# RWKV slot: half of the b Gram product copied by ScalarE, level one's dx in another bank, the v turn first, GpSimd's building a level later

## The chip, the cores and the metric

The program runs on one core of a Trainium2 chip (trn2). The metric is the device time of one launch in microseconds (us), the median of several runs. TensorE (PE) does the matrix products into PSUM, VectorE (DVE), ScalarE (ACT) and GpSimd (POOL) work beside it, and SyncE (SP) issues the loads of the weights. Each engine takes its instructions in the order in which they are written; semaphores hold the engines together.

## The reference, cut to what matters

The model is two blocks of two layers each over 256 tokens of 1024 columns. The change touches only one mixer of the first block, RWKV-7, and within it only the scan over time:

```python
def frame_step(state, inp):
    r_t, w_t, k_t, v_t, a_t, b_t = inp
    sa = jnp.einsum('bhvk,bhk->bhv', state, a_t)
    state = (state * w_t[:, :, None, :]
             + sa[..., None] * b_t[:, :, None, :]
             + v_t[..., None] * k_t[:, :, None, :])
    y_t = jnp.einsum('bhvk,bhk->bhv', state, r_t)
    return state, y_t
```

It is run for 16 heads of 64 columns, in 4 chunks of 64 tokens. The projections before it, the gate, the output product and the MLP behind it are large matrix products.

## The kernel before

The scan is done by chunks instead of by tokens. Within a chunk the dependence of the tokens on each other is a unit lower triangular matrix; its inverse is made first, for all chunks at once, and then a short chain goes from chunk to chunk with the state. Four heads (two pairs, called q = 0 and q = 1) make a **slot**, and there are four slots (`SLOTS`). A fifth pass of the loop holds the last chain.

For a slot `s` there is a list of steps, the same on every engine (`WKV_STEPS`, L572 to L581):

- **gram**, q 0 and 1. TensorE makes the b Gram product (`acc[0]`, `acc[1]`, from `b_fm` and `ar`) at q = 0, and turns v into tokens there (`un`, the v turn); at q = 1 it makes the k Gram product (`acc[2]`, `acc[3]`, from `k_fm` and `ar`). VectorE reads the b Gram product of pair q: `xt` (L1992), the level-one matrix `n_m` (L1993), `xt` plus the unit matrix (L1994), the masked product `nb_t` (L1995, 512 columns), and the transpose `xn` (L1996). ScalarE copies v out (L1281).
- **tok**. TensorE turns b and k into tokens. VectorE masks the k Gram product into `nk_t` (L2000), twice. ScalarE makes the exponentials `w_cum` and `w_inv` of the next slot (`wkv_build`, L1140 and L1141).
- **levels** j = 1 to 5, each with t1 (q 0, 1) and dx (q 0, 1). TensorE: t1 = `n_m` times `xn` into `acc[q]`; ScalarE copies it to `t1` (L1287); TensorE: dx = `xt` times `t1` into the second half of bank `acc[2 + q]`; VectorE adds it into `xt` (L2005) and transposes (L2008). GpSimd makes the `n_m` of levels 2 to 5 from `nb_t` (L817).
- **chain** steps rhs, u, sy, of the slot before, set between these by `WKV_CHAIN_AFTER`. rhs (TensorE) also finishes the y of the chunk before; ScalarE copies it to `wkv_rhs` (L1293); u (TensorE) follows, ScalarE copies it to `wkv_u` (L1301); sy makes the new state and y. VectorE copies y out (`keep_y`, L1980 and L1982), and sy waits for that before it writes y again.

In the code below, a step such as t1 of level 2, pair 1 is ("t1", 2, 1); the text calls it t1 2/1. Since each engine has one order, a step is late when its own input is late or when the instruction ahead of it on its engine is.

GpSimd also builds the operands of the next slot, `b_fm` and `k_fm` (`build_bk`) and `ar` (`build_ar`), between the `n_m` of two levels. In slot 0, which has no chain, TensorE has the last weight units of v beside the levels (L2252 to L2254), and VectorE splits their weights into high and low parts (L1507) and prepares the inputs of later slots (L1882 to L1889).

Of the kernel before, what the change touches and what calls it, by code (L numbers as in the profile page):

```python
# [7 lines left out]
ALU = mybir.AluOpType  # L8
# [5 lines left out]
P = 128  # L14
# [86 lines left out]
def build(nc, A, out):  # L101

    with ExitStack() as ctx:
# [626 lines left out]
        def _(pool):  # L730
# [79 lines left out]
            for s in range(SLOTS):  # L810
                for j in WKV_LEVELS[1:]:
                    for q in range(2):
                        if j == 2:
                            pool.wait_ge(inv_ready, 12 * s + q + 1)
                        else:
                            pool.wait_ge(t1_done, 10 * s + 2 * (j - 3) + q + 1)
                        G.tensor_tensor(n_m[(j - 1) % 2][:, q, :, :], nb_t[s % 2][:, q, :, 0:CHUNK],  # L817
                                        level_t[:, j, :].unsqueeze(1).to_broadcast([P, CHUNKS, CHUNK]), ALU.mult).then_inc(nm_ready, 1)
                    if j == (2 if s else 4) and s + 1 < SLOTS:
                        build_bk(s + 1)  # L820
                    if j == (3 if s else 5) and s + 1 < SLOTS:
                        build_ar(s + 1)
# [43 lines left out]
        def _(act):  # L866
# [618 lines left out]
        def _(dve):  # L1485
# [499 lines left out]
            for slot in range(SLOTS + 1):  # L1985
                for n, (step, s, j, q) in enumerate(wkv_steps(slot)):
                    xt, xn = inv_t[SLOT_SET[s]][:, q, :, :], inv_x[:, q, :, :]
                    if step == "gram":

                        dve.wait_ge(g_done, s + 1)  # L1990
                        raw_n = acc[q][:, :, :].rearrange("p a s -> p (a s)").rearrange("p (c q) -> p c q", c=CHUNKS)
# [5 lines left out]
                    elif step == "tok":  # L1997

                        dve.wait_ge(gk_done, s + 1)
                        V.tensor_tensor(nk_t[s % 2][:, q, :, :], bank4(acc[2 + q]), bc4(c_("masks"), CHUNKS), ALU.mult).then_inc(lak_ready, 1)  # L2000
                    elif step == "dx":
# [3 lines left out]
                        ins = V.tensor_tensor(x_, late(flat(acc[2 + q])[:, 2 * P:4 * P], j), x_, ALU.add)  # L2005
# [3 lines left out]
                        ins.then_inc(inv_ready, 1)  # L2009
                    elif step == "sy":  # L2010
# [236 lines left out]
        def _(pe):  # L2247
# [403 lines left out]
            for slot in range(SLOTS + 1):  # L2651
                for n, (step, s, j, q) in enumerate(wkv_steps(slot)):
# [3 lines left out]
                    if step == "gram":  # L2656
                        if q == 0:
                            pe.wait_ge(built, s + 1)
                            pe.wait_ge(const_mid_in, 16)
                            if s:  # L2660
                                pe.wait_ge(t1_out, 10 * s)
# [4 lines left out]
                            for c in range(CHUNKS):  # L2666
                                for m in range(2):
                                    ins = by_head(bank4(acc[m])[:, c, :], b_fm[:, m, c, :], ar[r_][:, m, c, :], cross=m == 1)
                            ins.then_inc(g_done, 1)
# [4 lines left out]
                            ins.then_inc(v_done, 1)  # L2674
                        else:
                            pe.wait_ge(inv_ready, 12 * s)
# [20 lines left out]
                    elif step == "dx":  # L2697
                        if j == 1:
                            pe.wait_ge(lak_ready, 2 * s + q + 1)
                        pe.wait_ge(t1_out, 10 * s + 2 * (j - 1) + q + 1)  # L2700
                        for c in range(CHUNKS):
                            ins = by_head(late(half_bank(acc[2 + q], 1)[:, c, :], j), t1[:, q, c, :], late(xt[:, c, :], j))
                        ins.then_inc(dx_done, 1)
                    else:
# [4 lines left out]
                        if step == "rhs":  # L2709
                            if c == 0:  # L2710
                                pe.wait_ge(inv_ready, 12 * s + 12)
                                pe.wait_ge(tok_out, 4 * s + 4)
                                pe.wait_ge(lak_ready, 2 * s + 2)
# [314 lines left out]
```

## Time and profile before

| | us |
|---|---|
| median of 3 runs | 1351.38 |
| lowest, highest | 1350.61, 1351.99 |
| profiled execution, its span | 1350.7 |
| the four slots and the last chain (427 to 550) | 123 |
| TensorE busy over the span | 1303.9 (97%) |
| VectorE busy | 948.4 (70%) |
| ScalarE busy | 701.1 (52%) |
| GpSimd busy | 128.3 (9%) |

A row of the timeline has the start in us, the length in us (of a row of several instructions, from the first's start to the last's end), engine, line, operation, output and inputs, shape and count; in brackets stands how long the engine had been idle, and what ended that. TensorE's rows count two instructions where the program has one in 32-bit arithmetic. TensorE's granted clock was 0.998 of its full level (2.4 GHz) on average, and is no part of what follows.

### The profile page before, as it was taken

What the parts mean: (1) busy time and instruction counts of PE and PEld (TensorE: products, weight loads), DVE (VectorE), ACT (ScalarE), POOL (GpSimd) and SP (SyncE); (2) the same over time, 40 slices, a digit from 0 to 9 for tenths busy, and PEclk for the clock granted to TensorE, in tenths of its full rate; (3) what the DMA queues carried; (4) which work ended last, traced back from release to release, by engine and by line L of the source; (5) the groups of instructions that cost most, each with busy time, mean ns of one, the idle gap of its engine ahead of it and who ended that gap; (6) DMA issues with size and microseconds to landing.
All of it is one profiled execution on the core that took longest, in us unless ns stands there. A gap on an engine that the chain in (4) does not pass through costs nothing. (4 is left out here: it accounts for less than half of the span.)

```text
span 1350.7 us, 24951 instructions
## 1 busy us (share of the span) xinstructions
PE 1303.9 (97%) x10507; PEld 1130.7 (84%) x10507; DVE 948.4 (70%) x1433; ACT 701.1 (52%) x1211; POOL 128.3 (9%) x133
## 2 busy tenths in 40 slices
PE   4999999999999999999999999999999999999997
PEld 2998888997899887788888887888888998888886
DVE  1887788976768776685556888666657677756655
ACT  2534544434467455564444648654445566644443
POOL 0000000010200864100000142000000021000000
PEclk9999999999999999999999999999999999999999
DMA  9997899995341012356665532465565544565561
GB/s 363 373 366 236 302 350 381 356 344 161 110 156 64 4 35 97 98 178 196 188 192 177 176 121 74 150 203 192 187 196 160 170 143 126 172 188 192 183 197 51
DMA packets 177559, 256.90 MB, mean 190 GB/s; under 512 B 10472, under 2 KB 122536, under 8 KB 177448
## 3 DMA queue, kind: packets, MB, share of 16 engines
q1 hardware_dynamic: 177448, 255.31, 57.0%
q8 instruction: 83, 1.36, 0.4%
q14 instruction: 28, 0.23, 0.0%
HBM read 254.25 MB, written 1.05 MB: 189 GB/s over the span
## 5 line engine op out<-in xcount | busy, mean ns | idle before, releaser
L1507 DVE TENSOR_TENSOR w_lo<-stage,w_hi 128x1024 fp32r<-128x1024 f32 (+1 forms) x372 | 447.3, 1238 | 160.4 <-ACT w_hi L882 160.0
L882 ACT ACTIVATE w_hi<-stage 128x1024 fp32r<-128x1024 f32 (+1 forms) x378 | 379.9, 1049 | 211.7 <-PE acc L2311 191.9
L2309 PE MATMUL acc<-w_hi,z_hi 128*128 128x512 f32 x640 | 252.7, 395 | 1.6 <-DVE z_lo L1956 1.6
L2311 PE MATMUL acc<-w_hi,z_lo 128*128 128x512 f32 x640 | 249.4, 390 | 0.0
L2310 PE MATMUL acc<-w_lo,z_hi 128*128 128x512 f32 x640 | 249.2, 389 | 0.0
L2252 PE MATMUL un<-h_both,w_hi 128*128 128x256 f32 x736 | 214.9, 292 | 1.8 <-POOL w_lo L853 1.1
L2253 PE MATMUL un<-h_both,w_hi 128*128 128x256 f32 x736 | 208.8, 284 | 0.0
L2254 PE MATMUL un<-h_both,w_lo 128*128 128x256 f32 x736 | 208.8, 284 | 0.0
L2252 PEld LDWEIGHTS un<-h_both,w_hi 128*128 128x128 f32 x736 | 141.6, 192 | 9.5 <-issue 5.4
L2309 PEld LDWEIGHTS acc<-w_hi,z_hi 128*128 128x128 f32 x640 | 120.1, 188 | 27.8 <-issue 3.9
L2253 PEld LDWEIGHTS un<-h_both,w_hi 128*128 128x128 f32 x736 | 141.7, 193 | 1.2 <-issue 0.7
L2254 PEld LDWEIGHTS un<-h_both,w_lo 128*128 128x128 f32 x736 | 141.7, 193 | 0.0
L2311 PEld LDWEIGHTS acc<-w_hi,z_lo 128*128 128x128 f32 x640 | 120.1, 188 | 25.4
L2310 PEld LDWEIGHTS acc<-w_lo,z_hi 128*128 128x128 f32 x640 | 120.2, 188 | 23.4
L2290 PE MATMUL un<-h_both,w_hi 128*128 128x512 f32 x384 | 121.2, 397 | 0.4 <-DVE w_lo L1507 0.4
L2290 PE MATMUL side<-h_both,w_hi 128*128 128x512 f32 x384 | 120.8, 396 | 0.4
L2293 PEld LDWEIGHTS side<-h_both,w_lo 128*128 128x128 f32 x384 | 72.1, 188 | 17.0
L2293 PEld LDWEIGHTS un<-h_both,w_lo 128*128 128x128 f32 x384 | 72.1, 188 | 16.9
L2293 PE MATMUL un<-h_both,w_lo 128*128 128x256 f32 x384 | 75.5, 278 | 0.0
L2293 PE MATMUL side<-h_both,w_lo 128*128 128x256 f32 x384 | 75.5, 278 | 0.0
L1789 DVE SCALAR_TENSOR_TENSOR ada_sum<-ada_buf,small,ada_sum 128x1024 f32<-128x1024 f32 x49 | 62.8, 1282 | 1.0
L2290 PEld LDWEIGHTS un<-h_both,w_hi 128*128 128x128 f32 x384 | 59.1, 189 | 1.7 <-DVE w_lo L1507 0.6
(393 smaller groups left out, 1885.1 us busy)
## 6 DMA issues: line engine op xcount, KB each, us to landing
stage<-in_mlp_w SPq DMA_DIRECT2D x64, 1024.0 KB
ada_buf<-in_ada_w SPq DMA_DIRECT2D x48, 1024.0 KB, 11.1
stage<-in_w_up SPq DMA_DIRECT2D x32, 1024.0 KB
stage<-in_w_down SPq DMA_DIRECT2D x32, 1024.0 KB
stage<-in_conv_w_in SPq DMA_DIRECT2D x12, 1024.0 KB
stage<-in_rw_w_rkv SPq DMA_DIRECT2D x12, 1024.0 KB
stage<-in_w_in_a SPq DMA_DIRECT2D x8, 1024.0 KB
stage<-in_w_kv_b SPq DMA_DIRECT2D x8, 1024.0 KB
```

The costliest lines, as they stand in the source:

```text
L882: A_(w_hi[u % 2][:, half, 0:n], stage[u % NSTAGE][:, half, 0:n], ACT.Copy).then_inc(hi_made, 1)
L1507: V.tensor_tensor(w_lo[u % 2][:, half, 0:n], stage[u % NSTAGE][:, half, 0:n], w_hi[u % 2][:, half, 0:n].bitcast(F32), ALU.subtract).then_i ...
L1789: V.scalar_tensor_tensor(out=to[:], in0=rows, scalar=by, in1=to[:], op0=ALU.mult, op1=ALU.add).then_inc(ada_weighed, 1)
L2252: MM(out, hi_l, hi_r, start=start, stop=False, skip_group_check=True)
L2253: MM(out, hi_l, lo_r, start=False, stop=False, skip_group_check=True)
L2254: return MM(out, lo_l, hi_r, start=False, stop=stop, skip_group_check=True)
L2290: MM(pair[:, m, :, :], wh[:, kt, c], h_both[:, kt, :, :], start=(kt == 0), stop=False, skip_group_check=True)
L2293: ins = MM(pair[:, m, 0, :], wl[:, kt, c], h_hi[:, kt, :], start=False, stop=(kt == KT - 1), skip_group_check=True)
L2309: MM(y, z_hi[:, kt, q], wh[:, i, :], start=(first and kt == 0), stop=False, skip_group_check=True)
L2310: MM(y, z_hi[:, kt, q], wl[:, i, :], start=False, stop=False, skip_group_check=True)
L2311: ins = MM(y, z_lo[:, kt, q], wh[:, i, :], start=False, stop=(last and kt == KT - 1), skip_group_check=True)
```

## The change

- **v turn first.** TensorE makes the v turn ahead of the b Gram product. The b Gram product now waits for `inv_ready` (VectorE's last addition of the slot before), where it had waited for ScalarE's last copy of t1.
- **Half of the b Gram product by ScalarE.** Columns 0 to 63 of each chunk of `nb_t` are no longer masked by VectorE but copied unmasked by ScalarE, pair 1 as soon as the Gram product is there, pair 0 after VectorE has made `xt` and `n_m` from it. VectorE masks only the other half, and for pair 0 it waits for ScalarE's copy. Both v copies of ScalarE stand ahead of it.
- **Level one's dx** goes to the second half of `acc[q]`, and the masking of k (`nk_t`) is moved from ahead of level one to behind each of its additions. TensorE's wait for it is at dx of level two.
- **`wkv_build`** on ScalarE is moved behind level one's copies.
- **GpSimd** starts level two's `n_m` at ScalarE's copies, and in slots 1 and 2 it builds b and k behind level three's `n_m` and ar behind level four's (before: level two's and three's).

```diff
 # GpSimd
                         if j == 2:
-                            pool.wait_ge(inv_ready, 12 * s + q + 1)
+                            pool.wait_ge(tok_out, 4 * s + 2)
...
-                    if j == (2 if s else 4) and s + 1 < SLOTS:
+                    if j == (3 if s else 4) and s + 1 < SLOTS:
                         build_bk(s + 1)
-                    if j == (3 if s else 5) and s + 1 < SLOTS:
+                    if j == (4 if s else 5) and s + 1 < SLOTS:
                         build_ar(s + 1)
 # ScalarE
                     if step == "gram":
-                        act.wait_ge(v_done, s + 1)
-                        act.wait_ge(lo_made, 2 * (BESIDE_SLOT[0] + 1))
-                        A_(v_tok[SLOT_SET[s]][:, q, :, :], half_bank(un[q], 1), ACT.Copy).then_inc(tok_out, 1)
-                    elif step == "tok":
-                        if q == 1 and s + 1 < SLOTS:
-                            wkv_build(s + 1)
+                        if q == 0:
+                            act.wait_ge(v_done, s + 1)
+                            act.wait_ge(lo_made, 2 * (BESIDE_SLOT[0] + 1))
+                            for m in range(2):
+                                A_(v_tok[SLOT_SET[s]][:, m, :, :], half_bank(un[m], 1), ACT.Copy)
+                            act.wait_ge(g_done, s + 1)
+                        else:
+                            act.wait_ge(lak_ready, 3 * s + 1)
+                        A_(nb_t[s % 2][:, 1 - q, :, 0:CHUNK], bank4(acc[1 - q])[:, :, 0:CHUNK], ACT.Copy).then_inc(tok_out, 1)
...
+                            if q == 1 and s + 1 < SLOTS:
+                                wkv_build(s + 1)
 # VectorE
-                        link(V.tensor_tensor(n_m[0][:, q, :, :], raw_n[:, :, 0:CHUNK], bc4(level_t[:, 1, :], CHUNKS), ALU.mult))
+                        ins = V.tensor_tensor(n_m[0][:, q, :, :], raw_n[:, :, 0:CHUNK], bc4(level_t[:, 1, :], CHUNKS), ALU.mult)
+                        if q == 0:
+                            ins.then_inc(lak_ready, 1)
+                            dve.wait_ge(lak_ready, 3 * s + 1)
+                        else:
+                            link(ins)
                         V.tensor_tensor(xt, xt, bc4(eye, CHUNKS), ALU.add)
-                        link(V.tensor_tensor(nb_t[s % 2][:, q, :, :], raw_n, bc4(c_("masks"), CHUNKS), ALU.mult))
+                        dve.wait_ge(tok_out, 4 * s + 2)
+                        link(V.tensor_tensor(nb_t[s % 2][:, q, :, CHUNK:2 * CHUNK], raw_n[:, :, CHUNK:2 * CHUNK], bc4(c_("masks")[:, CHUNK:2 * CHUNK], CHUNKS), ALU.mult))
...
-                        ins = V.tensor_tensor(x_, late(flat(acc[2 + q])[:, 2 * P:4 * P], j), x_, ALU.add)
+                        ins = V.tensor_tensor(x_, late(flat(acc[q if j == 1 else 2 + q])[:, 2 * P:4 * P], j), x_, ALU.add)
...
+                        if j == 1:
+                            dve.wait_ge(gk_done, s + 1)
+                            V.tensor_tensor(nk_t[s % 2][:, q, :, :], bank4(acc[2 + q]), bc4(c_("masks"), CHUNKS), ALU.mult).then_inc(lak_ready, 1)
 # TensorE
-                        if j == 1:
-                            pe.wait_ge(lak_ready, 2 * s + q + 1)
+                        if j == 2:
+                            pe.wait_ge(lak_ready, 3 * s + q + 2)
```

TensorE between slot 1 and slot 2, `un<-const,rw` being the v turn, `ar,b_fm` and `ar,k_fm` the Gram products, `side<-...` chain steps. Before:

```order
L2642 MATMUL acc<-inv_t_128,t_152 64x32 x16
L2642 MATMUL acc<-ar_191,b_fm 64x128 x16
L2642 MATMUL un<-const_64,rw_113 64x64 x16
L2642 MATMUL side<-v_tok_127,nk_t_136 64x64 x4
L2642 MATMUL acc<-ar_191,k_fm 64x128 x16
```

And after:

```order
L2654 MATMUL acc<-inv_t_128,t_152 64x32 x16
L2654 MATMUL un<-const_64,rw_113 64x64 x16
L2654 MATMUL acc<-ar_191,b_fm 64x128 x16
L2654 MATMUL side<-v_tok_127,nk_t_136 64x64 x4
L2654 MATMUL acc<-ar_191,k_fm 64x128 x16
```

The v turn and the b Gram product have changed places; nothing else has on this engine.

VectorE in slot 1, from the second pair's level-one matrix to level one's additions (L1995 and L2000 of before are the two maskings). Before:

```order
L1995 TENSOR_TENSOR nb_t_134<-acc,const_64 128x512
L1996 STREAM_TRANSPOSE inv_x<-inv_t_128 128x256 [waits dve_chain]
L2020 TENSOR_SCALAR state_146<-side,w_end 128x64 [waits s_done]
L2020 TENSOR_SCALAR state_146<-side,w_end 128x64
L2000 TENSOR_TENSOR nk_t_136<-acc,const_64 128x512 [waits gk_done] x2
L2005 TENSOR_TENSOR inv_t_128<-acc,inv_t_128 128x64x2 [waits dx_done]
L2008 STREAM_TRANSPOSE inv_x<-inv_t_128 128x256 [waits dve_chain]
L1980 COPY tmp<-side 128x64 [waits y_done]
L1982 COPY tmp<-side 64x64 x2
L2005 TENSOR_TENSOR inv_t_128<-acc,inv_t_128 128x64x2 [waits dx_done]
```

And after:

```order
L2008 TENSOR_TENSOR nb_t_134<-acc,const_64 128x4x64 [waits tok_out]
L2009 STREAM_TRANSPOSE inv_x<-inv_t_128 128x256 [waits dve_chain]
L2032 TENSOR_SCALAR state_146<-side,w_end 128x64 [waits s_done]
L2032 TENSOR_SCALAR state_146<-side,w_end 128x64
L2014 TENSOR_TENSOR inv_t_128<-acc,inv_t_128 128x64x2 [waits dx_done]
L2017 STREAM_TRANSPOSE inv_x<-inv_t_128 128x256 [waits dve_chain]
L2021 TENSOR_TENSOR nk_t_136<-acc,const_64 128x512 [waits gk_done]
L1985 COPY tmp<-side 128x64 [waits y_done]
L1987 COPY tmp<-side 64x64 x2
L2014 TENSOR_TENSOR inv_t_128<-acc,inv_t_128 128x64x2 [waits dx_done]
```

The masking of the b product has half its columns and a wait; the masking of k has moved from ahead of the first addition to between that and the copies of y.

ScalarE in slot 1, level one. Before:

```order
L1290 ACTIVATE bk_tok_129<-un 128x512 [waits tok_done]
L1293 ACTIVATE wkv_rhs<-side 128x128 [waits rhs_done]
L1298 ACTIVATE state_kept<-state_146,w_end 128x64 [waits state_ready]
L1298 ACTIVATE state_kept<-state_146,w_end 128x64
L1301 ACTIVATE wkv_u<-side 128x128 [waits u_done]
```

And after:

```order
L1293 ACTIVATE bk_tok_129<-un 128x512 [waits tok_done]
L1140 ACTIVATE w_cum<-rw_114 128x512 [waits built]
L1141 ACTIVATE w_inv<-rw_114 128x512
L1298 ACTIVATE wkv_rhs<-side 128x128 [waits rhs_done]
L1303 ACTIVATE state_kept<-state_146,w_end 128x64 [waits state_ready]
L1303 ACTIVATE state_kept<-state_146,w_end 128x64
L1306 ACTIVATE wkv_u<-side 128x128 [waits u_done]
```

The two exponentials now stand ahead of the chain's copy.

## Rows read from the trace of the kernel before

**Rows 1.** Timeline, VectorE, slot 2: start, length, engine, line, operation.

```profile
478.58 0.29 DVE L2005 TENSOR_TENSOR inv_t<-acc,inv_t 128x128 f32<-128x128 f32 x1 [0.41 <-PE acc L2642]
479.52 0.42 DVE L1992 TENSOR_TENSOR inv_t<-acc,const 128x256 f32<-128x256 f32 x1 [0.65 <-PE acc L2642]
479.86 0.41 DVE L1993 TENSOR_TENSOR n_m<-acc,const 128x256 f32<-128x256 f32 x1
...
480.65 0.68 DVE L1995 TENSOR_TENSOR nb_t<-acc,const 128x512 f32<-128x512 f32 x1
481.37 0.45 DVE L1996 STREAM_TRANSPOSE inv_x<-inv_t 128x256 f32<-128x256 f32 x1
...
484.26 1.28 DVE L2000 TENSOR_TENSOR nk_t<-acc,const 128x512 f32<-128x512 f32 x2
```

**Rows 2.** Timeline, TensorE, slot 1.

```profile
462.18 0.68 PE L2642 MATMUL acc<-inv_x,n_m 64*64 64x64 f32 x16 [1.50 <-DVE inv_x L1996]
...
464.01 0.45 PE L2642 MATMUL side<-wkv_rhs,inv_t 64*64 64x64 f32 x8
...
465.46 0.45 PE L2642 MATMUL side<-v_tok,bk_tok 64*64 64x64 f32 x8
...
466.44 0.63 PE L2642 MATMUL acc<-inv_x,n_m 64*64 64x64 f32 x16
```

**Rows 3.** Timeline, TensorE, slot 2.

```profile
478.37 1.07 PE L2642 MATMUL acc<-ar,b_fm 64*64 64x128 f32 x30
479.19 0.71 PE L2642 MATMUL un<-const,rw 64*64 64x64 f32 x32
...
483.92 0.40 PE L2642 MATMUL un<-const,b_fm 64*64 64x64 f32 x12 [1.51 <-issue]
```

**Rows 4.** Timeline, VectorE, slot 1.

```profile
456.26 1.43 DVE L1507 TENSOR_TENSOR w_lo<-stage,w_hi 128x1024 fp32r<-128x1024 f32 x1 [0.62 <-ACT w_hi L882]
...
464.95 0.46 DVE L1982 COPY tmp<-side 64x64 f32<-64x64 f32 x2
```

**Rows 5.** Timeline, ScalarE, slot 1.

```profile
458.23 0.62 ACT L1140 ACTIVATE w_cum<-rw 128x512 f32<-128x512 f32 x1
458.75 0.62 ACT L1141 ACTIVATE w_inv<-rw 128x512 f32<-128x512 f32 x1
...
463.67 0.28 ACT L1293 ACTIVATE wkv_rhs<-side 128x128 f32<-128x128 f32 x1
```

**Rows 6.** Timeline, ScalarE, slot 0.

```profile
431.84 0.36 ACT L1281 ACTIVATE v_tok<-un 128x256 f32<-128x256 f32 x1
```

**Rows 7.** Timeline, TensorE, slot 0.

```profile
436.37 0.39 PE L2252 MATMUL side<-h_both,w_hi 128*128 128x256 f32 x1
```

**Rows 8.** Timeline, VectorE, slot 0.

```profile
433.86 2.34 DVE L1507 TENSOR_TENSOR w_lo<-stage,w_hi 128x1024 fp32r<-128x1024 f32 x2
...
441.46 0.29 DVE L2005 TENSOR_TENSOR inv_t<-acc,inv_t 128x128 f32<-128x128 f32 x1 [1.88 <-PE acc L2642]
...
444.89 0.29 DVE L2005 TENSOR_TENSOR inv_t<-acc,inv_t 128x128 f32<-128x128 f32 x1 [0.67 <-PE acc L2642]
```

**Rows 9.** DMA queues from 481.0 to 481.5: packets, MB, share of 16 engines.

```profile
q1 hardware_dynamic: 80, 0.13, 69.0%
q8 instruction: 1, 0.02, 12.4%
```

**Rows 10.** Timeline, VectorE, slot 3.

```profile
503.33 0.49 DVE L2005 TENSOR_TENSOR inv_t<-acc,inv_t 128x128 f32<-128x128 f32 x2
504.25 0.42 DVE L1992 TENSOR_TENSOR inv_t<-acc,const 128x256 f32<-128x256 f32 x1 [0.44 <-PE acc L2642]
...
505.04 1.13 DVE L1994 TENSOR_TENSOR inv_t<-inv_t,const 128x256 f32<-128x256 f32 x1
```

**Rows 11.** Timeline, GpSimd, slots 1 and 3.

```profile
468.07 1.27 POOL L776 TENSOR_TENSOR ar<-rw,w_cum 128x512 f32<-128x512 f32 x1
...
504.61 1.29 POOL L783 TENSOR_TENSOR rw<-rw,rw 128x512 f32<-128x512 f32 x1
```

More of the change, by code:

```diff
@@ L1990, in _ @@
                         dve.wait_ge(g_done, s + 1)
+                        if q:
+                            dve.wait_ge(tok_out, 4 * s + 1)
                         raw_n = acc[q][:, :, :].rearrange("p a s -> p (a s)").rearrange("p (c q) -> p c q", c=CHUNKS)
                         V.tensor_tensor(xt, raw_n[:, :, 0:CHUNK], bc4(level_t[:, 0, :], CHUNKS), ALU.mult)
-                        link(V.tensor_tensor(n_m[0][:, q, :, :], raw_n[:, :, 0:CHUNK], bc4(level_t[:, 1, :], CHUNKS), ALU.mult))
+                        ins = V.tensor_tensor(n_m[0][:, q, :, :], raw_n[:, :, 0:CHUNK], bc4(level_t[:, 1, :], CHUNKS), ALU.mult)
[4 more added lines that the diff above has]
+                            link(ins)
                         V.tensor_tensor(xt, xt, bc4(eye, CHUNKS), ALU.add)
-                        link(V.tensor_tensor(nb_t[s % 2][:, q, :, :], raw_n, bc4(c_("masks"), CHUNKS), ALU.mult))
+                        dve.wait_ge(tok_out, 4 * s + 2)
+                        link(V.tensor_tensor(nb_t[s % 2][:, q, :, CHUNK:2 * CHUNK], raw_n[:, :, CHUNK:2 * CHUNK], bc4(c_("masks")[:, CHUNK:2 * CHUNK], CHUNKS), ALU.mult))
                         V.transpose(in_line(xn), in_line(xt)).then_inc(inv_ready, 1)
-                    elif step == "tok":
-                        dve.wait_ge(gk_done, s + 1)
-                        V.tensor_tensor(nk_t[s % 2][:, q, :, :], bank4(acc[2 + q]), bc4(c_("masks"), CHUNKS), ALU.mult).then_inc(lak_ready, 1)
                     elif step == "dx":
@@ L2659, in _ @@
                             pe.wait_ge(const_mid_in, 16)
-                            if s:
-                                pe.wait_ge(t1_out, 10 * s)
                             pe.wait_ge(tok_out, 4 * s)
@@ L2665, in _ @@
                                 pe.wait_ge(bonus_ready, s - 2)
[L2666 to L2669, printed above, removed]
                             v = rw_v[:, 2 * s:2 * s + 2, :].rearrange("p m (c s) -> p m c s", c=CHUNKS)
@@ L2674, in _ @@
                             ins.then_inc(v_done, 1)
+                            if s:
+                                pe.wait_ge(inv_ready, 12 * s)
+                            for c in range(CHUNKS):
+                                for m in range(2):
+                                    ins = by_head(bank4(acc[m])[:, c, :], b_fm[:, m, c, :], ar[r_][:, m, c, :], cross=m == 1)
+                            ins.then_inc(g_done, 1)
                         else:
-                            pe.wait_ge(inv_ready, 12 * s)
                             for c in range(CHUNKS):
@@ L2697, in _ @@
                     elif step == "dx":
-                        if j == 1:
-                            pe.wait_ge(lak_ready, 2 * s + q + 1)
+                        if j == 2:
+                            pe.wait_ge(lak_ready, 3 * s + q + 2)
                         pe.wait_ge(t1_out, 10 * s + 2 * (j - 1) + q + 1)
                         for c in range(CHUNKS):
-                            ins = by_head(late(half_bank(acc[2 + q], 1)[:, c, :], j), t1[:, q, c, :], late(xt[:, c, :], j))
+                            ins = by_head(late(half_bank(acc[q if j == 1 else 2 + q], 1)[:, c, :], j), t1[:, q, c, :], late(xt[:, c, :], j))
                         ins.then_inc(dx_done, 1)
@@ L2712, in _ @@
                                 pe.wait_ge(tok_out, 4 * s + 4)
-                                pe.wait_ge(lak_ready, 2 * s + 2)
+                                pe.wait_ge(lak_ready, 3 * s + 3)
                                 pe.wait_ge(un_free, freed(V_RKV + 11))
```

## The prediction

> **What bounds the kernel now.** I read the page's busy shares, then the timelines of VectorE, TensorE and ScalarE of each slot, in this order, looking at what ended each engine's idle time. The change lies wholly in the 123 us from 427 to 550 us; behind that stand products bound by TensorE (97% busy over the span), so I pass a shift of the slots' end on to the end at one to one. Within a slot of 1 to 3 there are two stretches. In the **first** TensorE has little to do and VectorE sets the pace: it starts on the b Gram product (479.52 in slot 2) and takes 2.2 us per pair until the transpose is out [rows 1]. t1 1/1 needs the second pair's transpose; in slot 1 TensorE is idle for 1.50 us for it and starts at 462.18 [rows 2]. In the **second**, from there to the next slot, TensorE's steps follow each other nearly without a gap; there the chain's small copies on ScalarE and VectorE only have to come in time. So a gain must come ahead of t1 1/1, and every delay of a copy behind it can spend the gain.
>
> **The masking by halves** takes VectorE's L1995 from 512 columns to 256. Before, it takes 0.72 us from its start to the transpose's (480.65 to 481.37); the same engine's read of 256 columns of the same bank takes 0.41, and with the wait for its end I take 0.44, so 0.28 saved per pair [rows 1]. For pair 0 there is a new wait: ScalarE may copy only after L1993. L1993 starts at 479.86 and its successor could start 0.45 later; a ScalarE copy of 256 columns from PSUM takes 0.36 [rows 6], and with about 0.06 for each semaphore it ends at about +0.5, while the addition of the unit matrix ends at +0.4. So 0.1 is lost again. The saving is 0.28 + 0.18, say **0.45 us per slot** in slots 1 to 3. In slot 0 it is worth nothing, as TensorE has v's weight units to do. Bounds: 0.2 (ScalarE late by another 0.25) to 0.56.
>
> **Masking k later** saves nothing ahead of level one: in slot 1 VectorE had idle time between that masking and the first addition, and TensorE was in t1 1/1 and rhs. Where it goes, it costs. The two maskings take 0.64 us each [rows 1]. The first now stands ahead of the copies of y, and sy (465.46) starts 0.05 us after those end (464.95 + 0.46) [rows 2, 4]; so y's release comes 0.64 later, less the 0.45 gained. In slots 2 and 3 the bonus product (L2618, 256 columns wide) stands between dx 1/0 and u, which covers it. In slot 0 there is no chain, but the additions wait for VectorE: ahead of level two's first addition it had 0.67 us of idle time [rows 8], and it gets 1.28 more work. That is **+0.6 us in slot 0**; bounds 0.2 (TensorE's part of a weight unit between the levels covers most) and 1.2 (if VectorE's two-input preparations then meet GpSimd's building).
>
> **ScalarE in slot 0** has the copy of pair 0 behind the four-part inverse norms, so it starts at about 431.9 instead of at 429.5 [rows 6], and VectorE waits there for 2.4 us. Its second pair then ends at about 435.0, and its weight split, before at 433.86, starts there [rows 8]. TensorE wants the split's first half at 436.37 [rows 7]; 435.0 + 1.17 = 436.2 comes just in time. VectorE's later preparations have 1.88 us of idle time ahead of 441.46 to give [rows 8]. I put it at 0; without that cover it costs what exceeds 0.2 us, one to one.
>
> **wkv_build later.** The exponentials start 0.52 us apart and last 0.62 [rows 5], so a copy behind them is late by 1.04. In slot 1 the chain's rhs copy stands at 463.67 [rows 5]; it becomes 463.67 - 0.45 + 1.04 = 464.26, 0.59 later, and u, at 464.01 only just behind that copy [rows 2], goes to 464.6. Queued behind u on TensorE are dx 1/1, t1 2/0, sy, t1 2/1. There were small gaps between them; walking them down gives t1 2/0 +0.5, sy 465.84 in place of 465.46, t1 2/1 466.82 in place of 466.44. So slot 1 ends **+0.4** instead of -0.45. In slot 2 the bonus product covers the exponentials; slot 3 has none; in slot 0 they come between two levels where ScalarE is idle. Bounds for slot 1: -0.45 (if rhs copy and y are hidden) and +0.8.
>
> **v turn first.** Before, the b Gram product ran while VectorE made its last addition (478.58 to 478.87) [rows 1, 3]. Now the v turn (32 matmuls, some 0.55 us of issue) goes first and the Gram product waits for that addition: start 478.93 instead of 478.26, VectorE's start 0.67 later. In slot 1 this is hidden: VectorE is in a weight split until 457.6 [rows 4], and the Gram product is there at 456.8. In slot 2 it gives 0.67 - 0.45 = +0.2; but TensorE then stood for 1.51 us with cause "issue" until 483.92 [rows 3], and a packet of instructions came in behind the last packets of a weight load [rows 9]. I read this as the program being fetched late. The load's time hangs on the chain of slot 0 and the fetch sits at the same place of the program, so the stall's end stays, t1 1/1 stays behind it, and I take **0** for slot 2 (bounds -1.1, the stall gone, and +0.7). In slot 3 the addition ends at 503.82 and VectorE started at 504.25 [rows 10]: +0.8. Against it stand the 0.45, and L1994, which took 1.13 us beside GpSimd's L783 in place of 0.42 [rows 10, 11]: 0.8 us later it meets the gap behind L783. I take **+0.1** (bounds -0.5 and +0.5).
>
> The Trainium skill ("Runtime: NRT & Kernel Launch", Instruction fetch mechanics) says that the refill of instructions is mostly hidden; the 1.51 us row differs. By the page alone slot 2 would have nothing to hide its +0.2 behind, and the sum would be 0.2 larger.
>
> **GpSimd's building later.** The `n_m` it must deliver come earlier; nothing waits for the building itself, which ends 6 us and more ahead of the next slot in slot 1 (468.07 + 1.27 [rows 11], Gram product at 478.3 [rows 3]). But in slot 1 its last piece, 1.27 us, now falls at about 469.8 to 471.0, onto VectorE's weight split at 470.0 to 471.3. L1994 shows that a two-input operation of VectorE can stand for the rest of a GpSimd operation, there 0.7 us [rows 10, 11]. Level three's additions have 0.2 us to spare behind that split. I take **+0.1**, bounds 0 and +0.4 in each of slots 1 and 2.
>
> That is what the Trainium skill says too ("SBUF — State Buffer", SBUF: two separate sides): the port pair shared by VectorE and GpSimd is held for a whole instruction, and the other blocks fully. By that rule taken strictly the split would wait until 471.0, and the slot would lose 0.4 in place of 0.1; the trace has both, L1994's 1.13 and a split of 1.43 in [rows 4] against 1.17 each in [rows 8].
>
> **Sum**: 0.6 + 0.4 + 0 + 0.1 + 0.1 = +1.2 us on the profiled span of 1350.7, so 1351.9; the median lies 0.7 above that span, so **1352.6**. By about 0.2% (2.7 us) a measurement of this kernel can tell a change from none; this is below it.
>
> **Rivals.**
> 1. *The covers hold*: k's masking and the exponentials lie in idle time, and slots 1 to 3 each keep 0.45, with L1994's 0.7 on top: 1351.38 - 1.35 - 0.7 = 1349.3. For it: VectorE was idle for 0.4 to 0.7 us ahead of many additions [rows 1, 8]. Against: sy stood 0.05 behind y's copies, and u 0.06 behind rhs's copy. 24%.
> 2. *The fetch stall goes too*: another 1.1, 1348.2, faster by over 0.2%. Against: the load and the place of the fetch stay. 4%.
> 3. *Slower, by VectorE standing behind GpSimd*: building and `n_m` are moved against VectorE's weight splits and slot 0's preparations. Three operations of 1.27 us that each block VectorE fully, on top of +1.2, give up to +5.0; with two thirds of it 1354.7. It decides when a split starts after a GpSimd piece, from 0.2 us of blocking on. 11%.
> 4. *Nothing*: the stage is bound by TensorE's issue anyhow, 1351.4. It differs from the forecast by less than can be told; 5%.
>
> **How the numbers follow.** The forecast (0 to +2.7) has 56%, rivals 1 to 4 have 24, 4, 11 and 5%. Below 1349.3 there are some 8%, above 1354.8 some 8%: the range is 1349.3 to 1354.8. Faster by over 0.2% is rival 2, 0.04; slower rival 3, 0.11; within it the rest, 0.85.
>
> **What would show it.** From VectorE's start on the Gram product to its second transpose's end: 3.95 us, before 4.4. Gram product to VectorE in slots 2 and 3: later by 0.7 and 0.8 behind the last addition. The rhs copy of slot 1 directly behind `w_inv`, u waiting for it. In slot 0 level two's addition later by 0.6. The "issue" gap in slot 2 still there. If t1 2/1 follows t1 1/1 in slot 1 within 4.3 us as before, and not 5.1, my main loss is wrong; if the stage ends more than 1 us before 550, rival 1 was right.

## The result and the profile after

| | before | after |
|---|---|---|
| median, us | 1351.86 | 1354.66 |
| profiled execution, its span, us | 1350.7 | 1353.7 |
| ratio after / before, with its 95% interval | | 1.0023 [1.0015, 1.0031] |

The changed kernel is slower, by 2.8 us between the medians (13 runs of each) and by 3.1 us from the ratio: just over the 0.2% that a measurement can tell. One of the 13 executions of after took 1613.74 us at a granted clock of 0.755; such outliers are left out of every ratio here. The time lies within the range, but the forecast of +1.2 us is too small by more than half.

First the page of after, and then the row of the windows view for 427 to 550 us, once of before and once of after (columns: the stretch, its length, busy time of PE, PEld, DVE, ACT and POOL with their instructions, TensorE's granted clock, DMA share, GB/s).

```profile
span 1353.7 us, 24956 instructions
...
PE 1304.5 (96%) x10507; PEld 1131.0 (84%) x10507; DVE 948.8 (70%) x1433; ACT 704.1 (52%) x1219; POOL 128.3 (9%) x133
```

```profile
427.00:550.00 123.00, 115.99 (x2981) 104.18 (x2981) 90.57 (x225) 67.23 (x163) 70.48 (x70) 1.00 0.12 38
```

```profile
427.00:550.00 123.00, 114.29 (x2968) 102.32 (x2969) 90.03 (x222) 68.01 (x168) 67.64 (x68) 1.00 0.12 38
```

Over the span only ScalarE has noticeably more work (3.0 us, its copies). The same 123 us hold 1.7 us less of TensorE's work: the loss is waiting within the slots, and the clock has no part in it.

To place it, I read VectorE's timeline in both kernels at rows that both have, and count each from the weight split that stands ahead of slot 0. The first and last of these rows, before and then after:

```profile
425.46 2.35 DVE L1507 TENSOR_TENSOR w_lo<-stage,w_hi 128x1024 fp32r<-128x1024 f32 x2
...
549.54 1.91 DVE L1507 TENSOR_TENSOR w_lo<-stage,w_hi 128x1024 fp32r<-128x1024 f32 x1 [1.65 <-ACT w_hi L882]
```

```profile
425.44 2.35 DVE L1512 TENSOR_TENSOR w_lo<-stage,w_hi 128x1024 fp32r<-128x1024 f32 x2
...
552.22 1.92 DVE L1512 TENSOR_TENSOR w_lo<-stage,w_hi 128x1024 fp32r<-128x1024 f32 x1 [1.65 <-ACT w_hi L882]
```

That is 124.08 and 126.78 us: the **stage** is 2.70 us longer, nearly all of the 3.0 by which the spans differ. "Shift" below is such a mark of one kernel less the same mark of another. Between kernels with the same code up to a mark it repeats within 0.02 us, so it separates effects that the medians don't. Outside the stage the 13 profiled executions of before, after and the experiments differ by themselves: the stage starts at 425.4 to 427.5 us, and from its end to the program's end it takes 800.0 to 801.6 us, in no order that follows the change. Differences of 1 to 2 us between medians can come from there.

| mark | before | after | shift |
|---|---|---|---|
| slot 0, level two's first addition | 19.43 | 20.61 | +1.18 |
| slot 1, first read of the b Gram product | 32.15 | 33.60 | +1.45 |
| slot 1, addition 1/0 | 38.59 | 39.54 | +0.95 |
| slot 1, addition 2/0 | 42.10 | 43.79 | +1.69 |
| slot 1, addition 5/1 | 53.12 | 55.24 | +2.12 |
| slot 2, first read | 54.06 | 56.76 | +2.70 |
| slot 2, addition 1/0 | 61.48 | 63.20 | +1.72 |
| slot 2, addition 3/0 | 70.62 | 73.53 | +2.91 |
| slot 2, addition 5/0 | 77.87 | 80.77 | +2.90 |
| slot 3, first read | 78.79 | 82.49 | +3.70 |
| slot 3, addition 1/0 | 85.90 | 88.62 | +2.72 |
| end of the stage | 124.08 | 126.78 | +2.70 |

An addition is named as its dx is: 1/0 is that of level one, pair 0. So slot 0 lost 1.45, slot 1 0.67, slot 2 0.78, and slot 3 gave 0.20 back. The rows behind each:

**Slot 0.** VectorE after, behind level one's first addition.

```profile
442.05 0.65 DVE L2021 TENSOR_TENSOR nk_t<-acc,const 128x512 f32<-128x512 f32 x1
...
443.30 0.65 DVE L2021 TENSOR_TENSOR nk_t<-acc,const 128x512 f32<-128x512 f32 x1
443.88 1.00 DVE L1887 TENSOR_TENSOR tmp<-tmp,ss_inv 128x512 f32<-128x512 f32 x1
444.92 1.10 DVE L1888 SCALAR_TENSOR_TENSOR tmp<-tmp 128x512 f32<-128x512 f32 x1
446.05 0.29 DVE L2014 TENSOR_TENSOR inv_t<-acc,inv_t 128x128 f32<-128x128 f32 x1
```

The same two preparations before, with the addition of [rows 8] behind them at 444.89:

```profile
442.85 0.65 DVE L1882 TENSOR_TENSOR tmp<-tmp,ss_inv 128x512 f32<-128x512 f32 x1
443.53 0.69 DVE L1883 SCALAR_TENSOR_TENSOR tmp<-tmp 128x512 f32<-128x512 f32 x1
```

GpSimd at this place, before and then after:

```profile
443.73 1.77 POOL L817 TENSOR_TENSOR n_m<-nb_t,const 128x256 f32<-128x256 f32 x2 [2.10 <-PE acc L2642]
```

```profile
443.61 1.86 POOL L817 TENSOR_TENSOR n_m<-nb_t,const 128x256 f32<-128x256 f32 x2 [1.68 <-PE acc L2654]
```

The maskings took 1.2 us, and beyond that the preparations took 2.10 us instead of 1.34. Before, the first of them started 0.9 us ahead of GpSimd; now it starts 0.27 behind it.

**Slot 1.** After; ScalarE, then TensorE, where [rows 5] and [rows 2] stood before.

```profile
464.60 0.63 ACT L1140 ACTIVATE w_cum<-rw 128x512 f32<-128x512 f32 x1
465.11 0.63 ACT L1141 ACTIVATE w_inv<-rw 128x512 f32<-128x512 f32 x1
465.63 0.28 ACT L1298 ACTIVATE wkv_rhs<-side 128x128 f32<-128x128 f32 x1
```

```profile
463.11 0.68 PE L2654 MATMUL acc<-inv_x,n_m 64*64 64x64 f32 x16 [0.84 <-DVE inv_x L2009]
...
465.96 0.45 PE L2654 MATMUL side<-wkv_rhs,inv_t 64*64 64x64 f32 x8 [1.03 <-ACT wkv_rhs L1298]
...
468.11 0.63 PE L2654 MATMUL acc<-inv_x,n_m 64*64 64x64 f32 x16
```

The chain's copy stands behind the exponentials, and TensorE waits 1.03 us for it.

**Slots 1 and 2, the weight splits.** After, VectorE and GpSimd in slot 1 (two fences), then in slot 2 (two).

```profile
471.76 1.66 DVE L1512 TENSOR_TENSOR w_lo<-stage,w_hi 128x1024 fp32r<-128x1024 f32 x1 [0.33 <-ACT w_hi L882]
```

```profile
471.06 1.28 POOL L776 TENSOR_TENSOR ar<-rw,w_cum 128x512 f32<-128x512 f32 x1
```

```profile
496.72 2.22 DVE L1512 TENSOR_TENSOR w_lo<-stage,w_hi 128x1024 fp32r<-128x1024 f32 x1 [0.33 <-ACT w_hi L882]
```

```profile
495.16 1.28 POOL L776 TENSOR_TENSOR ar<-rw,w_cum 128x512 f32<-128x512 f32 x1
496.59 1.27 POOL L794 TENSOR_TENSOR rw<-tmp,rw 128x512 f32<-128x512 f32 x1 [0.15 <-POOL ar L776]
```

And before, in slot 2:

```profile
494.75 1.30 DVE L1507 TENSOR_TENSOR w_lo<-stage,w_hi 128x1024 fp32r<-128x1024 f32 x1 [0.33 <-ACT w_hi L882]
```

```profile
492.95 1.27 POOL L794 TENSOR_TENSOR rw<-tmp,rw 128x512 f32<-128x512 f32 x1
494.24 2.40 POOL L817 TENSOR_TENSOR n_m<-nb_t,const 128x256 f32<-128x256 f32 x2
```

The splits grew from 1.25 to 1.66 and from 1.30 to 2.22 us. In slot 2 it is not the building that does it but L794, which stands behind the building in GpSimd's queue: it is pushed from well ahead of the split to 0.13 us ahead of it.

**Slots 2 and 3, their heads.** After: VectorE, TensorE's gap in slot 2, and VectorE in slot 3 (for [rows 1], [rows 3] and [rows 10]).

```profile
480.68 0.29 DVE L2014 TENSOR_TENSOR inv_t<-acc,inv_t 128x128 f32<-128x128 f32 x1 [0.41 <-PE acc L2654]
482.20 0.42 DVE L1999 TENSOR_TENSOR inv_t<-acc,const 128x256 f32<-128x256 f32 x1 [1.23 <-PE acc L2654]
...
485.78 0.45 DVE L2009 STREAM_TRANSPOSE inv_x<-inv_t 128x256 f32<-128x256 f32 x1
```

```profile
485.67 0.40 PE L2654 MATMUL un<-const,b_fm 64*64 64x64 f32 x12 [1.05 <-issue]
```

```profile
507.93 0.42 DVE L1999 TENSOR_TENSOR inv_t<-acc,const 128x256 f32<-128x256 f32 x1 [1.23 <-PE acc L2654]
...
508.72 0.42 DVE L2006 TENSOR_TENSOR inv_t<-inv_t,const 128x256 f32<-128x256 f32 x1
```

The Gram product comes 0.57 us later behind the last addition (1.52 for 0.94) and from VectorE's start on it to its second transpose's end the turn takes 4.03 us (485.78 + 0.45 - 482.20); counted alike it was 4.48 before, so 0.45 less. The gap by "issue" is 1.05 instead of 1.51, and the addition of the unit matrix in slot 3 takes 0.42 us (L2006), where L1994 took 1.13.

### The profile page after: what moved, and what is told of

Its sections match the earlier page's. It is cut to its first block and busy times, and to the rows that moved or that the text cites. A ratio compares the mean times of both kernels' runs of the same rounds, so it can differ in the third digit from the quotient of the medians.

```text
span 1353.7 us, 24956 instructions
## 1 busy us (share of the span) xinstructions
PE 1304.5 (96%) x10507; PEld 1131.0 (84%) x10507; DVE 948.8 (70%) x1433; ACT 704.1 (52%) x1219; POOL 128.3 (9%) x133
## 3 DMA queue, kind: packets, MB, share of 16 engines
q8 instruction: 83, 1.36, 0.4%
HBM read 254.25 MB, written 1.05 MB: 189 GB/s over the span
```

## The experiments

Two theories stood after the result. **A**: the loss is in the three steps that were moved later (k's masking, the exponentials, GpSimd's building), in slot 0 by way of the masking; half the b Gram product on ScalarE is itself a gain. **B**: the loss comes from the new way of the b Gram product (the v turn ahead of it, ScalarE's copies and the waits for them). The first kernels undo one part of the change each, the later ones start from a kernel with all three steps back and put one in again. Each was measured beside before on the same chip; "kept" is the change as it stands, and lines with + are what the experiment puts in.

| kernel | median | ratio to before | stage | slot 1's first read | slot 1's split | slot 2's split | gap by "issue" |
|---|---|---|---|---|---|---|---|
| before | 1351.86 | 1 | 124.08 | 32.15 | 1.25 | 1.30 | 1.51 |
| after | 1354.66 | 1.0023 [1.0015, 1.0031] | 126.78 | 33.60 | 1.66 | 2.22 | 1.05 |
| e1 | 1354.12 | 1.0019 [1.0010, 1.0028] | 126.30 | 33.13 | 1.65 | 2.23 | 1.02 |
| e2 | 1354.36 | 1.0018 [1.0009, 1.0027] | 125.89 | 33.60 | 1.47 | 2.03 | 0.93 |
| e3 | 1353.92 | 1.0017 [1.0008, 1.0025] | 126.26 | 33.60 | 1.66 | 1.63 | 1.06 |
| e4 | 1357.69 | 1.0040 [1.0027, 1.0053] | 127.58 | 33.99 | 1.67 | 2.21 | 1.29 |
| e7 | 1354.34 | 1.0016 [1.0007, 1.0025] | 127.11 | 33.61 | 1.66 | 2.23 | 1.34 |
| e8 | 1352.81 | 1.0007 [0.9998, 1.0016] | 125.29 | 32.09 | 1.66 | 2.22 | 1.06 |
| e9 | 1350.79 | 0.9989 [0.9980, 0.9998] | 123.02 | 32.08 | 1.30 | 1.32 | 1.06 |
| e10 | 1350.40 | 0.9983 [0.9974, 0.9992] | 123.18 | 32.08 | 1.30 | 1.30 | 1.36 |
| e11 | 1351.60 | 1.0000 [0.9990, 1.0009] | 124.29 | 32.09 | 1.47 | 2.02 | 1.48 |
| e12 | 1352.31 | 1.0010 [1.0000, 1.0020] | 124.96 | 32.08 | 1.65 | 1.63 | 1.34 |
| e13 | 1351.07 | 0.9999 [0.9990, 1.0009] | 124.12 | 32.07 | 1.30 | 1.31 | 1.61 |

### e1: k masked ahead of level one again

```diff
 # VectorE
+                    elif step == "tok":
+                        dve.wait_ge(gk_done, s + 1)
+                        V.tensor_tensor(nk_t[s % 2][:, q, :, :], ...).then_inc(lak_ready, 1)
 # and out of "dx", j == 1
```

> The changed kernel with one part undone: VectorE masks the k Gram product ahead of level one again, in all slots. Theory A (the loss of slot 0 is the k masking pushing VectorE's preparations under GpSimd's operations): in slot 0 level two's first addition is 1.1 us earlier (at about 444.9 again), and slot 1's first read of the b Gram product 1.4 us earlier (about 457.6); the kernel gains about 1.4 us on the changed one, ratio to the kernel before about 1.001. Theory B (the loss sits in TensorE's new order and waits): slot 0 as in the changed kernel, gain under 0.3 us.

The stage is 0.48 us shorter, a third of what was expected, and slot 0 is not cured: slot 1's first read comes only 0.47 earlier. In slot 0 the masking now stands ahead of the weight split, and that had no slack left: VectorE had waited 2.37 us for ScalarE's copy, which stands behind the inverse norms. The split starts at mark 10.69 (before 8.40), and TensorE waits for it:

```profile
437.62 0.38 PE L2264 MATMUL side<-h_both,w_hi 128*128 128x256 f32 x1 [0.97 <-DVE w_lo L1512]
```

So the two edits cover each other: the late copy costs nothing only as long as k's masking is not in front of that split.

### e2: the exponentials early

```diff
 # ScalarE
+                    elif step == "tok":
+                        if q == 1 and s + 1 < SLOTS:
+                            wkv_build(s + 1)
 # and out of "t1", j == 1, q == 1
```

> The changed kernel with one part undone: ScalarE makes the next slot's two exponentials ahead of level one again. Theory A: in slot 1 TensorE's step u no longer waits 1.03 us for the rhs copy; t1 of level two, pair one, follows t1 of level one, pair one, within 4.3 us in place of 5.0; in slot 2 another 0.2 to 0.3; gain on the changed kernel about 1.0 us. Rival: the y copies behind the k masking hold the chain just as long, and the gain is under 0.4 us.

-0.89 for the stage, near the 1.0 expected, but most of it not where expected. In slot 1 u no longer waits for the rhs copy, but sy then waits 0.50 for the copies of y, and t1 2/1 comes 4.85 behind t1 1/1 where 4.3 was expected. Addition 1/1 didn't move (k's masking stands ahead of the copies of y, which hold it), addition 2/0 gained 0.15 and the split 0.19; in slot 2 the stretch from addition 1/0 to 3/0 went from 10.33 to 9.86, 0.19 of it the split. The medians (1354.36 for 1354.66) do not tell it from after.

### e3: GpSimd's building early

```diff
 # GpSimd
-                    if j == (3 if s else 4) and s + 1 < SLOTS:
+                    if j == (2 if s else 4) and s + 1 < SLOTS:
                         build_bk(s + 1)
-                    if j == (4 if s else 5) and s + 1 < SLOTS:
+                    if j == (3 if s else 5) and s + 1 < SLOTS:
                         build_ar(s + 1)
```

> The changed kernel with one part undone: GpSimd builds b, k behind level two's matrices and ar behind level three's again in slots 1 and 2. Theory A (VectorE's weight splits of slots 1 and 2 stand behind the building): the splits take 1.3 us each in place of 1.66 and 2.22, gain about 1.3 us. Theory B: the splits are as short, but the time is the same within 0.3 us, as TensorE's stream hides it. If the building then waits longer for the late exponentials, level three's matrices come late and it is slower than the changed kernel by up to 1 us.

-0.52 instead of the 1.3 expected, and slot 2's split (1.63 for 2.22) accounts for it. Slot 1's split stayed at 1.66: the building is first in its queue but waits for the exponentials, which are still late. VectorE in slot 2, and GpSimd in slot 1 and in slot 2:

```profile
498.59 1.63 DVE L1512 TENSOR_TENSOR w_lo<-stage,w_hi 128x1024 fp32r<-128x1024 f32 x1 [0.33 <-ACT w_hi L882]
```

```profile
467.72 1.27 POOL L761 TENSOR_TENSOR b_fm<-rw,w_inv 128x512 f32<-128x512 f32 x1 [4.17 <-ACT w_inv L1141]
...
498.41 2.39 POOL L817 TENSOR_TENSOR n_m<-nb_t,const 128x256 f32<-128x256 f32 x2
```

### e4: the b Gram product ahead of the v turn

```diff
 # TensorE, "gram", q == 0 (ScalarE's order kept: v's copies ahead)
+                            if s:
+                                pe.wait_ge(t1_out, 10 * s)
+                            (the b Gram product)
                             (the v turn)
 # "gram", q == 1
+                            pe.wait_ge(inv_ready, 12 * s)
```

> The changed kernel with one part undone: TensorE makes the b Gram product ahead of the v turn, waiting for ScalarE's last copy only. Theory A: VectorE's start in slots 2 and 3 comes 0.6 and 0.8 us earlier behind the last addition; slot 2's is lost in the instruction stall, slot 3 keeps 0.3 to 0.8; gain 0.3 to 0.8 us. Theory B (the order on TensorE is the main loss): gain 1.5 us or more.

A gain was expected, and the stage lost another 0.80. The median is 3.0 above after's, of 5 runs only; the execution profiled was the shortest of them and its span is after's (1353.6 for 1353.7), so what the median has beyond the 0.80 no trace shows. Of the 0.80, 0.39 came in slot 0 (slot 1's first read at 33.99 for 33.60). In slot 2 the first read comes 0.93 us behind slot 1's last addition instead of 1.52, but then VectorE waits for ScalarE, whose copy of pair 1 still stands behind v's copies, and the gap by "issue" is 0.24 longer. VectorE in slot 2, and ScalarE:

```profile
484.43 0.42 DVE L2008 TENSOR_TENSOR nb_t<-acc,const 128x256 f32<-128x256 f32 x1 [0.66 <-ACT nb_t L1287]
```

```profile
483.01 0.66 ACT L1283 ACTIVATE v_tok<-un 128x256 f32<-128x256 f32 x2 [1.50 <-PE un L2654]
483.98 0.41 ACT L1287 ACTIVATE nb_t<-acc 128x256 f32<-128x256 f32 x1
```

The v turn first belongs to ScalarE's order; one is not to be judged without the other.

### e7 and e8: slot 0

e7: ScalarE's copy of pair 0 in slot 0 stands ahead of the inverse norms.

```diff
 # ScalarE, "gram"
-                        else:
+                        elif s:
                             act.wait_ge(lak_ready, 3 * s + 1)
-                        A_(nb_t[s % 2][:, 1 - q, ...
+                        if s or q == 0:
+                            A_(nb_t[s % 2][:, 1 - q, ...
+                        if s == 0 and q == 0:
+                            act.wait_ge(lak_ready, 1)
+                            A_(nb_t[0][:, 0, :, 0:CHUNK], bank4(acc[0])[:, :, 0:CHUNK], ACT.Copy).then_inc(tok_out, 1)
```

> The changed kernel, but in slot 0 ScalarE copies pair 0 ahead of the inverse norms. Theory A (slot 0's loss is the 1.3 us of k masking between level one's additions, which pushes VectorE's two-input preparations under GpSimd's building): VectorE no longer waits 2.4 us in slot 0, but level two's first addition stays 1.1 us late; gain under 0.3 us. Theory B (slot 0's loss is that wait): level two's first addition is back where it was, gain 1.1 to 1.4 us.

e8 is e7 with k masked ahead of level one in slot 0 alone (the edit of e1 with `and s == 0`).

> As e7_copy0_first, and in slot 0 alone VectorE masks k ahead of level one. Theory A: wait and masking are each other's cover, and only both undone bring slot 0 back: slot 1's first read of the b Gram product 32.2 us behind VectorE's weight split at 425.5 as before the change, in place of 33.6; gain on the changed kernel 1.4 us. Theory B: no more than e7_copy0_first.

e7 alone gained nothing in slot 0 (first read of slot 1 at 33.61; the split is early, at 8.33, but level two's addition is where it was, 20.62); its stage is 0.33 longer than after's, 0.29 of it in the gap by "issue". e8 put slot 0 where it was before: 19.42 and 32.09. Its preparations run ahead of GpSimd again:

```profile
444.81 0.65 DVE L1891 TENSOR_TENSOR tmp<-tmp,ss_inv 128x512 f32<-128x512 f32 x1
445.50 0.69 DVE L1892 SCALAR_TENSOR_TENSOR tmp<-tmp 128x512 f32<-128x512 f32 x1
446.93 0.29 DVE L2021 TENSOR_TENSOR inv_t<-acc,inv_t 128x128 f32<-128x128 f32 x1 [0.74 <-PE acc L2661]
```

The stage is 1.49 shorter than after's, the first difference that the medians show too (1352.81). So all of slot 0's loss is k's masking behind level one; half the product on ScalarE costs slot 0 nothing, once its copy is early.

### e9 and e10: only the b Gram product's new way

e9 is e8 with the edits of e1, e2 and e3: of the change the half on ScalarE, the v turn first and level one's dx in `acc[q]` are left. e10 is e9 with the b Gram product first (e4), and ScalarE's copies of v behind its copy of pair 1:

```diff
 # ScalarE, "gram", q == 0
-                            act.wait_ge(v_done, s + 1)
                             act.wait_ge(lo_made, 2 * (BESIDE_SLOT[0] + 1))
-                            (v's two copies)
                             act.wait_ge(g_done, s + 1)
                         A_(nb_t[s % 2][:, 1 - q, ...
+                        if q == 0:
+                            act.wait_ge(v_done, s + 1)
+                            (v's two copies)
```

> The changed kernel with k masked early, the exponentials early, the building early, and slot 0's copy ahead of the inverse norms: what is left of the change is the half copy by ScalarE and the v turn first. Theory A (losses of the three moves add up: 1.4 + 0.4 + 0.9 + 0.5): back to the kernel before within 0.5 us, since the v turn first costs about what the half masking gains; 1351.4 to 1352.4 where the kernel before is at 1352.0. Rival: the loss is in the pair kept, and it stays 1.5 us or more above the kernel before.

> As e9_half_only_v_first, with the b Gram product ahead of the v turn again, and ScalarE's copy of pair 1 ahead of its v copies to match. If the half masking gives 0.45 us in each of slots 1 to 3 and nothing is paid for it, this is faster than the kernel before by 0.5 to 1.3 us; if ScalarE's copy of pair 0 comes late behind the v copies, VectorE waits for it and the gain is gone: within 0.3 us of the kernel before.

e9's stage is 123.02: 3.76 below after and 1.06 below before. Theory B falls, theory A stands: what is left of the change is a gain, more than was expected (within 0.5 us of before). Of the 1.06, 0.50 is there by the end of slot 1, 0.37 comes in slot 2, where the gap by "issue" is 0.45 shorter and the v turn first costs 0.58, and 0.19 in slot 3. e10 is as good (the stages differ by 0.16, and the intervals overlap): slot 2's first read comes 0.58 us earlier, and VectorE then waits 0.39 for ScalarE and TensorE's gap is 0.30 longer. VectorE in e10, slot 2:

```profile
480.61 0.43 DVE L2014 TENSOR_TENSOR nb_t<-acc,const 128x256 f32<-128x256 f32 x1 [0.39 <-ACT nb_t L1285]
```

Both have an interval wholly below 1: by the ratios they beat the kernel before by 1.5 and 2.3 us, and after by more. Which share of that the bank of level one's dx has was not tried.

### e11, e12 and e13: each late step put back singly

e9 with the building late (e3 undone), with the exponentials late (e2 undone), and with k's masking late in slots 1 to 3.

> e9_half_only_v_first with one move put back: GpSimd builds a level later in slots 1 and 2. Theory A (VectorE's splits stand behind the building): split in slot 1 1.5 to 1.7 us and in slot 2 about 2.2 in place of 1.30 and 1.32; the stage from VectorE's split at 425.5 to that at 549.5 grows from 123.0 to 124.2. Rival: TensorE's stream hides it, under 0.3 us.

> e9_half_only_v_first with one move put back: the exponentials behind level one's copies. Theory A: ScalarE's rhs copy in slot 1 is 1.0 us late and TensorE's u waits for it, +0.6 in slot 1, +0.2 to 0.3 in slot 2, and the building, which needs them, is pushed towards the splits: stage 123.0 to about 124.0. Rival: only together with the late k masking does it cost: under 0.3 us.

> e9_half_only_v_first with one move put back: k masked behind level one's additions in slots 1 to 3 (slot 0 early). Theory A: y's copies in slot 1 are 0.6 us later and sy waits for them, +0.4 to 0.6 in slot 1, nothing in slots 2 and 3, where the bonus product covers it: stage 123.0 to 123.5. Rival: nothing, within 0.1.

The stage is longer than e9's by 1.27, 1.94 and 1.10 us; 1.2, about 1.0 and up to 0.5 were expected. Walked along the marks:

- **Building** (e11): slot 1's split +0.17, slot 2's +0.70, the gap by "issue" +0.42 (1.48 for 1.06).
- **Exponentials** (e12): the chain in slot 1 +0.74 at addition 2/0 (42.26 for 41.52), the splits +0.35 and +0.31 (the building that waits for them), another 0.27 between additions 1/0 and 3/0 of slot 2, the gap +0.28. TensorE in slot 1, as in after:

```profile
464.44 0.45 PE L2658 MATMUL side<-wkv_rhs,inv_t 64*64 64x64 f32 x8 [1.03 <-ACT wkv_rhs L1302]
```

- **k's masking** (e13): 0.59 in slot 1, where sy waits for y's copy behind it, and the other 0.5 by the gap. TensorE, slots 1 and 2:

```profile
465.58 0.45 PE L2662 MATMUL side<-v_tok,bk_tok 64*64 64x64 f32 x8 [0.50 <-DVE tmp L1992]
...
484.33 0.40 PE L2662 MATMUL un<-const,b_fm 64*64 64x64 f32 x12 [1.61 <-issue]
```

Singly they sum to 4.31 us, together (e8 less e9) they cost 2.27. The larger part of the difference is the gap: it was 0.28 to 0.55 longer than e9's in each of the three, 1.25 in sum, and in e8 it is e9's 1.06. The steps themselves account for the rest: in e8 addition 2/0 of slot 1 comes 0.75 behind e9's, as with the exponentials alone, so k's 0.59 is hidden behind the 1.03 us wait; and the splits grow by 1.26 where singly they grew by 1.53. So the steps cover each other in part, and undoing one of them in e1 to e3 gave little.

## Why the prediction was too low, step by step

**Slot 0, k's masking: +0.6 predicted, +1.45 measured**, beyond the bound of 1.2. The step that failed is the working "0.67 us of idle time, and it gets 1.28 more work": it let the rest of VectorE's queue keep its lengths. The work added pushed the two preparations from 0.9 us ahead of GpSimd's `n_m` to behind it, and they took 0.76 more; 1.2 + 0.76 - 0.67 is 1.3 (0.7 above the prediction), the mark shows 1.18, and another 0.27 came until the next slot, with the slot's last two splits at 2.13 and 1.77 us. The bound named that meeting, but did not price it from rows.

**GpSimd's building: +0.1 predicted, 0.41 + 0.92 measured** on the splits. Two steps failed. In slot 1 the price was a mean between being blocked and not, since the prediction took the 1.43 us split of [rows 4] for one that was not, or only partly, blocked. It was as fully blocked as L1994: the operation of GpSimd that stood beside it was simply nearer its end (456.61).

```profile
455.57 1.04 POOL L784 TENSOR_TENSOR rw<-rw,vecT 128x512 f32<-128x512 f32 x1
```

In slot 2 no instruction of GpSimd's queue was walked down behind the building: L794 there has the largest single part, and exceeds the bound of 0.4. How exactly it goes can be told from all the kernels. The split takes 1.08 us plus what was left, at its start, of the GpSimd operation in progress:

| kernel, slot | split starts | GpSimd's operation ends | 1.08 + rest | measured |
|---|---|---|---|---|
| before, 1, the one of [rows 4] | 456.26 | L784, 456.61 | 1.43 | 1.43 |
| before, 2 | 494.75 | `n_m`, 494.97 | 1.30 | 1.30 |
| after, 1 | 471.76 | L776, 472.34 | 1.66 | 1.66 |
| after, 2 | 496.72 | L794, 497.86 | 2.22 | 2.22 |
| e2, 1 | 471.78 | L776, 472.17 | 1.47 | 1.47 |
| e3, 2 | 498.59 | `n_m`, 499.14 | 1.63 | 1.63 |
| e9, 2 | 494.08 | `n_m`, 494.32 | 1.32 | 1.32 |
| e11, 2 | 494.36 | L794, 495.31 | 2.03 | 2.02 |

(1.08 is fitted to these rows. A split beside an idle GpSimd takes 1.21, and the two of [rows 8] 2.34 together as they overlap; so being blocked costs some 0.13 less than the rest. The preparations of slot 0 fit the same: with rests of 0.46 and 0.55 they took 0.35 and 0.41 more than alone. The end of an `n_m` within a row of two is its start + 0.73, the length of one alone.) The other side pays as exactly: beside the split the two `n_m` of before took 2.40 instead of 1.41 us. In all these rows the one that starts first runs at full length.

The Trainium skill ("SBUF — State Buffer", SBUF: two separate sides) states just this for an operation of VectorE with two SBUF inputs against a GpSimd operation that reads SBUF: whichever starts first gets the shared pair for the whole instruction, and the other fully blocks. The prediction named the rule, worked out 0.4 from it for slot 1, and took 0.1; the measured 0.41 agrees with the rule.

**Slot 1, exponentials and y: right.** The rhs copy directly behind `w_inv`, u waiting for it, t1 2/1 5.00 us behind t1 1/1 (predicted 5.1, before 4.3). The turn gave 0.50 (predicted 0.45), the chain took 0.74 (0.85).

**Slot 2's head: about 0 predicted, -0.40 measured**, from the first row of the slot to addition 1/0, so within its bounds. The parts: +0.57 by the order of v turn and Gram product (0.67 predicted), -0.45 by the turn, -0.46 by a shorter gap, together -0.34. That the sum came near is luck, for the reason given was wrong: the gap's end did not stay where it was, it came 1.77 us later, with the slot. The weight load's time does not hang on slot 0 alone: SyncE issued it at mark 51.48 before and 53.60 after, 2.12 later, as much as slot 1's last addition. Before, then after:

```profile
476.94 0.39 SPq L637 DMA_DIRECT2D stage<-in_rw_w_o  x1
```

```profile
479.04 0.39 SPq L637 DMA_DIRECT2D stage<-in_rw_w_o  x1
```

And "in slot 2 the bonus product covers the exponentials" was wrong by 0.27 (e12).

**Slot 3: +0.1 predicted, -0.20 measured.** The Gram product came 0.80 later as predicted, the turn and L1994's 0.71 outweighed it.

**Slot 0, ScalarE: right as far as it went.** VectorE waited 2.37 us for the copy and no later mark shows it, as e7 confirms; e1 shows the price once the cover is gone.

Summed: 1.45 + 0.67 + 0.78 - 0.20 = 2.70, against 1.2. With strict blocking in both slots (+1.3 for 0.1) the sum would have been 2.4, with the preparations in slot 0 (+0.7) 3.1; the heads of slots 2 and 3 came out 0.7 better than forecast. **Rival 3** was the mechanism, to which I gave 11%: its place was right, its price came from two thirds of three operations, while the rows were there to price each. The gain of 0.45 per slot was real, and e9 shows it free of the rest.

## What to carry to other kernels

When work is moved on VectorE or GpSimd, walk both queues forward in time and look which of two overlapping operations now starts first; price the loser at the winner's whole rest, not at a mean. The pushed neighbour (here L794, and two preparations) can cost more than the step that was moved. A change of several parts is judged by taking them all back and putting them in singly, and also all together: undoing one of the three moves alone gave 0.5 to 0.9 us each here, since the others covered it, and put in alone they summed to 4.31 us where together they cost 2.27.

## What the runs showed of the hardware that I had not expected

TensorE's gap by "issue" in slot 2, in which a packet of instructions comes in behind a weight load [rows 9], is no fixed amount and no fixed time: it was 0.93 to 1.61 us in the 13 kernels of the table, whose code ahead of it is nearly the same, and its end, counted from the stage's start, lay between 57.6 (e9) and 61.1 us (e4). Slot 2's first read came at almost the same mark in before and e9 (54.06, 54.14), with 1.51 and 1.06 us of gap.

The DMA packets in the traces say what its end goes with. In all 13 kernels the load's packets run for 3.4 to 3.7 us, the 16 KB packet of instructions starts when they end (0 to 0.4 us ahead of the start of the load's last packet), though such packets are otherwise 3.4 to 5.3 us apart about there and this one comes 5.7 to 6.8 us behind the one before it, and TensorE goes on 2.2 to 2.5 us behind the packet's start (before: packet at mark 55.91, end of the gap at 58.45; after: 57.88 and 60.23; e9: 55.30 and 57.63). So a slot whose head takes longer, with the load issued at the same place, loses part of that in a shorter gap, and an early slot brings its load and the gap's end along. That the load holds the packet back is argued from these times; no run moved the load alone. The remaining 0.3 us between packet and end, and 0.4 us between load and packet, I can't predict from these rows.
